# The triangular solve of the RWKV mixer in 32 by 32 blocks on the four diagonal tiles of the array

## The chip, the cores and the metric

The kernel runs on one core of one Trainium2 chip. The metric is the device time in microseconds from the first to the last instruction of a run, lower is better.

## The reference, cut to what matters

A sequence of 256 tokens with 1024 features goes through four layers; the first begins with an RWKV-7 time mix of eight heads of 64 features. Its recurrence is

```python
def step(S, inp):
    r_t, w_t, k_t, v_t, kk_t, a_t = inp
    sa = jnp.einsum('bhvk,bhk->bhv', S, -kk_t)
    S = (S * w_t[:, :, None, :] + sa[..., None] * (kk_t * a_t)[:, :, None, :]
         + v_t[..., None] * k_t[:, :, None, :])
    return S, jnp.einsum('bhvk,bhk->bhv', S, r_t)
_, o = lax.scan(step, S0, (tm(rh), tm(wh), tm(kh), tm(vh), tm(kk), tm(ah)))
```

The kernel does it in two chunks of 128 tokens (n = 0, 1). In a chunk, the vectors sa of all tokens solve (I - L) sa = x with a strictly lower triangular L of 128 by 128 for each head. So the inverse T of a unit triangular matrix is wanted, for two chunks and eight heads. What stands behind it (attention, feed-forward layers with 22 tiles each, a second network) is the bulk of the kernel and is not touched.

## The kernel before, in words

Each engine has a program of its own, written out in order; semaphores tie them together. The function tensor_program issues the matmuls, vector_program and scalar_program copy results out of the eight PSUM banks, gpsimd_program fills buffers with zeros or unit matrices. A bank is opened for a key such as ("T", i, n) when its last reader is through (opened, read_out); bank_plan fixes which key has which bank.

The inverse is built by doubling. T starts as the unit matrix with the entries of L next to the diagonal (level 0). Level i doubles the size of the solved blocks: Y = L T is formed, only the part under the mask of the level is copied (VectorE, copy_predicated into a unit matrix), and T becomes T Y. The function blocks forms one such product for one chunk: for each of eight heads (g = 0, 1 and j = 0 to 3) two matmuls of 64 by 64 on the two diagonal tiles of the array, partitions 0 to 63 and 64 to 127. Levels 1 to 5 give the inverse of each block of 64. Two last products (keys Y64 and TT64) form the block of 64 by 64 that is left of 128, with L12, the part of L between the two halves. The level's steps are, on the engines:

- TensorE: Y for n = 0 and 1, then rest(i - 1), eight matmuls of 128 columns for products that the solve itself doesn't need, then T for n = 0 and 1.
- ScalarE: copies T to Tc (L1454). VectorE: copies Y (L1961), copies rest out (L1954), turns Tc into TTc in blocks of 32 by 32 (L1974). GpSimd: a fresh unit matrix into the buffer of Y.
- Level 5 forms T and its transpose TT (both by blocks), and copies TT into TTm, whose blocks the later products use.

Ahead of the levels stand the products for L (L2362, called gram below), the turned v (L2370), turned Bt and Kt (L2378) and cross (L2386), which makes L12. Behind the last level come Y64 (L2459), rest(5), X (L2441), TT64 (L2472), and then the first matmuls of the output projection (L1109), which fill the time between the small products.

All operands of the solve are f32; each such matmul stands in the trace as two records of TensorE (and two weight loads), so that 16 matmuls are 32 records. Matmuls of fp32r operands have one.

## Time and profile before

| | |
|---|---|
| median of 3 runs | 1253.51 us (1252.48 to 1256.44) |
| profiled execution, first to last instruction | 1253.0 us |
| its own device time | not given apart; its span is 0.5 us under the median of the runs |
| TensorE busy | 1230.9 us, 98% |
| solve, from gram to the first matmul of the output projection | 93.28 to 132.51 us |
| granted TensorE clock, mean | 0.999 |

Busy is the time in which at least one instruction of the engine runs. Matmuls overlap on the array, so a busy TensorE is not one at its peak; the pace is read from the starts and the counts of records.

### The profile page before, as it was taken

The page shows a single profiled execution, that of the slowest core. Times are in us where ns is not written, and L with a number is a line of the kernel's source. Part 1 is how long each engine was busy: PE and PEld are TensorE (multiplying, and loading weights), DVE is VectorE, ACT ScalarE, POOL GpSimd, SP SyncE. Part 2 cuts the span into 40 slices and gives each one's busy share as a digit, 9 for nine tenths or more (in the row PEclk, how much of TensorE's full clock was granted, in tenths as well). Part 3 has the DMA queues.
Part 4 walks back from the last instruction along what each step waited for, and adds up shares of the span by engine and source line. Part 5 has one row for each costly group of instructions (what it writes and reads, how often), then busy time and mean ns, then how long its engine had stood idle before and what let it go on. Part 6 is the DMA issues. An engine that isn't in the chain of part 4 may idle for free.

```text
span 1253.0 us, 23639 instructions
## 1 busy us (share of the span) xinstructions
PE 1230.9 (98%) x9987; PEld 1147.4 (92%) x9987; DVE 933.6 (75%) x1260; ACT 703.9 (56%) x1032; POOL 20.1 (2%) x31
## 2 busy tenths in 40 slices
PE   6999999999999999999999999999999999999998
PEld 6999889999999879999988998999998998999997
DVE  5888369888758777999987566899976666677453
ACT  6843477555555767666657556634445554643432
POOL 0002000000000000000000000000000000000000
PEclk9999999999999999999999999999999999999999
DMA  9450277776567256689653534899965356675540
GB/s 322 168 201 4 69 247 246 250 238 229 193 220 257 105 170 234 217 291 319 249 201 119 194 130 148 290 360 351 343 234 202 136 204 200 236 250 188 202 169 34
DMA packets 163683, 263.78 MB, mean 211 GB/s; under 512 B 5677, under 2 KB 98041, under 8 KB 163578
## 3 DMA queue, kind: packets, MB, share of 16 engines
q1 hardware_dynamic: 160586, 259.54, 60.3%
q10 hardware_dynamic: 2992, 2.72, 0.7%
q8 instruction: 79, 1.29, 0.4%
q14 instruction: 26, 0.21, 0.1%
HBM read 261.17 MB, written 1.05 MB: 209 GB/s over the span
## 4 chain that ended last, share of the span: by engine, by line
PE 97%; DVE 1%; ACT 1%; DMA 1%; issue 1%; SPq 0%; DVEq 0%; ACTq 0%
PE ps L1109 26%; PE ps L1080 17%; PE ps L1082 16%; PE ps L1081 16%; PE ps L847 2%; PE ps L848 2%; PE ps L849 2%; PE ps L1095 2%; PE ps L1097 2%; PE ps L1096 2%; PE ps L2397 2%; PE ps L827 1%; DMA ring<-in_ev_w_in_dram 1%; PE ps L2406 1%; PE ps L2597 1%
## 5 line engine op out<-in xcount | busy, mean ns | idle before, releaser
L623 DVE TENSOR_TENSOR wlo<-ring,whi 128x2048 fp32r<-128x2048 f32 x194 | 443.3, 2289 | 97.6 <-ACT whi L617 97.6
L1080 PE MATMUL ps<-ghi,whi 128*128 128x256 f32 x1600 | 449.0, 281 | 0.0
L1081 PE MATMUL ps<-glo,whi 128*128 128x256 f32 x1600 | 446.8, 279 | 0.0
L1082 PE MATMUL ps<-ghi,wlo 128*128 128x256 f32 x1600 | 446.5, 279 | 0.0
L617 ACT ACTIVATE whi<-ring 128x2048 fp32r<-128x2048 f32 x194 | 370.4, 1913 | 96.7 <-PE ps L1109 69.7
L1080 PEld LDWEIGHTS ps<-ghi,whi 128*128 128x128 f32 x1600 | 300.4, 188 | 2.0 <-DVE wlo L623 0.6
L1081 PEld LDWEIGHTS ps<-glo,whi 128*128 128x128 f32 x1600 | 299.7, 187 | 0.8
L1082 PEld LDWEIGHTS ps<-ghi,wlo 128*128 128x128 f32 x1600 | 300.4, 188 | 0.0
L1109 PE MATMUL ps<-whi,yhi 128*128 128x512 f32 x480 | 159.7, 396 | 0.7 <-DVE ylo L1996 0.7
L1109 PE MATMUL ps<-wlo,yhi 128*128 128x512 f32 x480 | 156.7, 390 | 0.0
L1109 PE MATMUL ps<-whi,ylo 128*128 128x512 f32 x480 | 156.6, 390 | 0.0
L1109 PEld LDWEIGHTS ps<-whi,ylo 128*128 128x128 f32 x480 | 90.1, 188 | 19.2
L1109 PEld LDWEIGHTS ps<-wlo,yhi 128*128 128x128 f32 x480 | 90.1, 188 | 18.9
L1109 PEld LDWEIGHTS ps<-whi,yhi 128*128 128x128 f32 x480 | 88.2, 188 | 20.3 <-issue 2.4
L2218 DVE SCALAR_TENSOR_TENSOR acc<-arena,small,acc 128x512 f32<-128x512 f32 x126 | 94.7, 751 | 6.4 <-DMA arena<-in_w_ada_dram 2.5
L2255 DVE SCALAR_TENSOR_TENSOR arena<-arena,cols 128x254 f32<-128x254 f32 (+1 forms) x176 | 73.9, 479 | 14.7 <-ACT arena L1770 14.2
L1774 ACT ACTIVATE arena<-ps 128x256 f32<-128x256 f32 x44 | 16.9, 384 | 111.8 <-PE ps L1082 111.8
L2270 DVE TENSOR_TENSOR ylo<-arena,yhi 128x256 fp32r<-128x256 f32 x88 | 37.1, 422 | 47.6 <-ACT yhi L1787 47.4
L847 PE MATMUL ps<-whi,ghi 128*128 128x256 f32 x224 | 63.5, 283 | 4.0 <-DVE glo L993 4.0
L1768 ACT ACTIVATE arena<-ps 128x512 f32<-128x512 f32 x44 | 26.3, 599 | 67.1 <-PE ps L1082 65.5
L849 PE MATMUL ps<-whi,glo 128*128 128x256 f32 x224 | 62.6, 279 | 0.0
L848 PE MATMUL ps<-wlo,ghi 128*128 128x256 f32 x224 | 62.5, 279 | 0.0
(314 smaller groups left out, 1575.0 us busy)
## 6 DMA issues: line engine op xcount, KB each, us to landing
arena<-in_w_ada_dram SPq DMA_DIRECT2D x48, 1024.0 KB, 6.0
ring<-in_ff_w_up_dram SPq DMA_DIRECT2D x44, 1024.0 KB, 7.6
ring<-in_w_gate_up_dram SPq DMA_DIRECT2D x44, 1024.0 KB, 7.5
ring<-in_ff_w_down_dram SPq DMA_DIRECT2D x10, 2048.0 KB, 7.9
ring<-in_w_down_dram SPq DMA_DIRECT2D x10, 2048.0 KB, 7.8
ring<-in_od_w_qkv_dram SPq DMA_DIRECT2D x6, 2048.0 KB, 8.6
ring<-in_w_qkv_dram SPq DMA_DIRECT2D x6, 2048.0 KB, 7.9
ring<-in_w_in_dram SPq DMA_DIRECT2D x6, 2048.0 KB, 8.1
```

Of the source, the lines that this page charges most:

```text
L617: e.activation(shaped(WHI[i % NB], k), v, ACT.Copy).then_inc(S["w_hi"], 1)
L623: e.tensor_tensor(shaped(WLO[i % NB], k), v, shaped(WHI[i % NB], k).bitcast(F32), ALU.subtract).then_inc(S["w_lo"], 1)
L847: e.matmul(o, h[0][:, c, t], wh, start=c == 0, stop=False)
L848: e.matmul(o, h[0][:, c, t], wl, start=False, stop=False)
L849: x = e.matmul(o, h[1][:, c, t], wh, start=False, stop=c == NK - 1)
L1080: e.matmul(o, wh, h[0][:, k, :], start=k == 0, stop=False)
L1081: e.matmul(o, wh, h[1][:, k, :], start=False, stop=False)
L1082: x = e.matmul(o, wl, h[0][:, k, :], start=False, stop=k == NK - 1)
L1109: x = e.matmul(ps[:, :], YT[l][:, src_k + i, t], w[r][:, i, 512 * h:512 * h + 512], start=first, stop=last)
L2218: e.scalar_tensor_tensor(a, AW[:, k, :], SC[:, k:k + 1], a, ALU.mult, ALU.add).then_inc(S["ada_acc"], 1)
L2255: e.scalar_tensor_tensor(t[a][:, lag:256], z[:, 256 * a:256 * a + 256 - lag], conv_col(f, 2 - lag, a * NF + p), t[a][:, lag:256], ALU.mult ...
L2270: e.tensor_tensor(YT[1][:, p % 8, :], tg[r], YT[0][:, p % 8, :].bitcast(F32), ALU.subtract).then_inc(S["y_lo"], 1)
```

## The change

Levels 1 to 4 only need blocks of 32, since a block of 64 appears first at level 5. So the function blocks now takes four matmuls of 32 by 32 for each head, one on each diagonal tile of the array (quarter), in place of two of 64 by 64. Tc, TTc, LTc and the buffers of Y are packed to half the columns (256 for a chunk), and copies and turns go over 256 columns. The products for L are made in blocks of 32 too. Level 5 is written out apart: cross also makes LX, the part of L between two neighbouring blocks of 32; last_y forms LX T for the two pairs, last_t forms only the block below the diagonal of T and of its transpose, and TT is no longer formed in full. Copies on ScalarE put the blocks of 32 together into T64 (for Y64) and TTm. rest(5) now stands ahead of Y64, and VectorE makes P2 at level 3 in place of level 5.

```diff
         for n in range(2):
             P.use(("T", i, n), r())
-            if i == 5:
-                P.use(("TT", i, n), r())
...
-        Tc, TTc, LTc = heads64(sv(41, 1024)), heads64(PR[:, 4224:5248]), heads64(PR[:, 0:1024])
-        Yb = [heads64(PR[:, 5312:6336]), heads64(PR[:, 1088:2112])]
+        def heads32(x):
+            return [x[:, 256 * n:256 * n + 256].rearrange("p (g j c) -> p g j c", g=2, j=4) for n in range(2)]
+
+        Tc, TTc, LTc = heads32(sv(41, 512)), heads32(PR[:, 4224:4736]), heads32(PR[:, 0:512])
+        Yb = [heads32(PR[:, 5312:5824]), heads32(PR[:, 1088:1600])]
+        LX = heads32(PR[:, 512:1024])
+        T64 = [PR[:, s:s + 512].rearrange("p (g j c) -> p g j c", g=2, j=4) for s in (4736, 5824)]
...
                 eye(flat64(TTc[n]), S["tt_eye"])
+            for n in range(2):
+                zeros64(n)
...
             for x in TTm:
-                e.memset(x[:, :, :, 0:64], 0.0).then_inc(S["tt_zero"], 1)
-            for i in (1, 2, 3):
+                e.memset(x[:, :, :, :], 0.0).then_inc(S["tt_set"], 1)
+            for i in (1, 2):
...
                     e.wait_ge(S["cross"], n + 1)
+                    e.wait_ge(S["tilted"], 6)
+                    for q in (0, 2):
+                        p = slice(32 * q, 32 * q + 32)
+                        e.activation(LX[n][p, g], c3(ps_of(key)[p, 256:384], 4), ACT.Copy)
                     e.activation(L12[n][0:64, g], c3(ps_of(key)[0:64, 0:256], 4), ACT.Copy).then_inc(bank_sem(key), 1)
...
+            def blocks_of(key):
+                return ps_of(key)[:, 0:256].rearrange("p (g j c) -> p g j c", g=2, j=4)
+
+            for i in range(1, 5):
                 for n in range(2):
                     key = ("T", i, n)
                     e.wait_ge(S["t_mm"], 2 * (i - 1) + n + 1)
-                    e.activation(Tc[n], heads_of(key), ACT.Copy).then_inc(bank_sem(key), 1)
-                    if i == 5:
-                        key = ("TT", i, n)
-                        e.wait_ge(S["tt_mm"], n + 1)
-                        ps = heads_of(key)
-                        e.wait_ge(S["tt_zero"], n + 1)
-                        e.activation(TTm[n][0:64, :, :, 0:64], ps[0:64], ACT.Copy)
-                        e.activation(TTm[n][64:128, :, :, 64:128], ps[64:128], ACT.Copy).then_inc(bank_sem(key), 1)
+                    e.activation(Tc[n], blocks_of(key), ACT.Copy).then_inc(bank_sem(key), 1)
+            def laid(n, q):
+                c = slice(32 * q, 32 * q + 32)
+                e.wait_ge(S["tt_set"], 2 + n + 1)
+                e.wait_ge(S["tt_turned"], 2 * 3 + n + 1)
+                e.activation(TTm[n][c, :, :, c], TTc[n][c], ACT.Copy).then_inc(S["tt_laid"], 1)
+
+            for n in range(2):
+                e.wait_ge(*read_out(("T", 4, n)))
+                e.wait_ge(S["tt_set"], 2)
+                for q in range(2):
+                    c = slice(32 * q, 32 * q + 32)
+                    e.activation(T64[n][c, :, :, c], Tc[n][c], ACT.Copy).then_inc(S["t64"], 1)
+            for n in range(2):
+                for q in (2, 3):
+                    laid(n, q)
+            for n in range(2):
+                key = ("T", 5, n)
+                ps = blocks_of(key)
+                e.wait_ge(S["t_mm"], 8 + n + 1)
+                e.activation(T64[n][32:64, :, :, 0:32], ps[32:64], ACT.Copy).then_inc(S["t64"], 1)
+                e.activation(TTm[n][64:96, :, :, 96:128], ps[64:96], ACT.Copy)
+                e.activation(TTm[n][0:32, :, :, 32:64], ps[0:32], ACT.Copy).then_inc(bank_sem(key), 1)
+            for n in range(2):
+                for q in (0, 1):
+                    laid(n, q)
...
-                    l, lt = (c3(ps_of(key)[:, 256 * i:256 * i + 256], 4) for i in range(2))
+                    l, lt = (c3(ps_of(key)[:, 128 * i:128 * i + 128], 4) for i in range(2))
                     e.wait_ge(S["gram"], n + 1)
                     e.wait_ge(S["t_eye"], n + 1)
                     e.wait_ge(S["tilted"], 6)
                     e.wait_ge(S["tt_eye"], 2 + n + 1)
-                    e.copy_predicated(LTc[n][:, g], mask64(C_S64, 4), lt)
-                    e.copy_predicated(Tc[n][:, g], mask64(C_Y64, 4), l)
-                    e.copy_predicated(TTc[n][:, g], mask64(C_P64, 4), lt).then_inc(bank_sem(key), 1)
+                    e.copy_predicated(LTc[n][:, g], mask32(C_S32, 4), lt)
+                    e.copy_predicated(Tc[n][:, g], mask32(C_Y32, 4), l)
+                    e.copy_predicated(TTc[n][:, g], mask32(C_P32, 4), lt).then_inc(bank_sem(key), 1)
...
             for i in range(1, 6):
                 for n in range(2):
-                    key = ("Y", i, n)
+                    key, y = ("Y", i, n), Yb[(i - 1) % 2][n].rearrange("p g j c -> p (g j) c")
                     e.wait_ge(S["y_mm"], 2 * (i - 1) + n + 1)
-                    e.wait_ge(S["y_eye"], 2 * (i - 1) + n + 1)
-                    e.copy_predicated(Yb[(i - 1) % 2][n].rearrange("p g j c -> p (g j) c"), mask64(C_Y64 + 64 * i, 8),
-                                      c3(ps_of(key)[:, :], 8)).then_inc(bank_sem(key), 1)
-                if i == 5:
+                    if i < 5:
+                        e.wait_ge(S["y_eye"], 2 * (i - 1) + n + 1)
+                        e.copy_predicated(y, mask32(C_Y32 + 32 * i, 8), c3(ps_of(key)[:, 0:256], 8)).then_inc(bank_sem(key), 1)
+                        continue
+                    for q in (1, 3):
+                        p = slice(32 * q, 32 * q + 32)
+                        x = e.tensor_copy(y[p], c3(ps_of(key)[p, 0:256], 8))
+                    x.then_inc(bank_sem(key), 1)
+                if i == 3:
...
+            quarter = [slice(32 * q, 32 * q + 32) for q in range(4)]
             e.wait_ge(S["tilted"], 3)
             for n in range(2):
                 ps = [opened(e, ("L", n, g)) for g in range(2)]
                 for j in range(4):
-                    for x, y, c in ((At, Bt, 0), (Bt, At, 256)):
-                        for b in range(2):
+                    for x, y, c in ((At, Bt, 0), (Bt, At, 128)):
+                        for p in quarter:
                             for g in range(2):
-                                z = e.matmul(ps[g][half[b], c + 64 * j:c + 64 * j + 64], x[half[g], j, n, half[b]],
-                                             y[half[g], j, n, half[b]], start=True, stop=True)
+                                z = e.matmul(ps[g][p, c + 32 * j:c + 32 * j + 32], x[half[g], j, n, p], y[half[g], j, n, p],
+                                             start=True, stop=True)
                 z.then_inc(S["gram"], 1)
...
                 ps = [opened(e, ("L12", n, g)) for g in range(2)]
                 for j in range(4):
                     for g in range(2):
-                        x = e.matmul(ps[g][half[0], 64 * j:64 * j + 64], Bt[half[g], j, n, half[0]],
-                                     At[half[g], j, n, half[1]], start=True, stop=True)
+                        e.matmul(ps[g][half[0], 64 * j:64 * j + 64], Bt[half[g], j, n, half[0]],
+                                 At[half[g], j, n, half[1]], start=True, stop=True)
+                for j in range(4):
+                    for q in (0, 2):
+                        for g in range(2):
+                            x = e.matmul(ps[g][quarter[q], 256 + 32 * j:288 + 32 * j], Bt[half[g], j, n, quarter[q]],
+                                         At[half[g], j, n, quarter[q + 1]], start=True, stop=True)
                 x.then_inc(S["cross"], 1)
 
...
                 ps = opened(e, key)
                 for g in range(2):
                     for j in range(4):
-                        c = 256 * g + 64 * j
-                        for b in range(2):
-                            x = e.matmul(ps[half[b], c:c + 64], l[half[b], g, j, :], r[half[b], g, j, :], start=True, stop=True)
+                        c = 128 * g + 32 * j
+                        for p in quarter:
+                            x = e.matmul(ps[p, c:c + 32], l[p, g, j, :], r[p, g, j, :], start=True, stop=True)
                 x.then_inc(sem, 1)
...
+            def last_y(n):
+
+                ps = opened(e, ("Y", 5, n))
+                for g in range(2):
+                    e.wait_ge(*read_out(("L12", n, g)))
+                for g in range(2):
+                    for j in range(4):
+                        c = 128 * g + 32 * j
+                        for q in (0, 2):
+                            x = e.matmul(ps[quarter[q + 1], c:c + 32], LX[n][quarter[q], g, j, :], Tc[n][quarter[q], g, j, :],
+                                         start=True, stop=True)
+                x.then_inc(S["y_mm"], 1)
+
+            def last_t(n, y):
+
+                ps = opened(e, ("T", 5, n))
+                for g in range(2):
+                    for j in range(4):
+                        c = 128 * g + 32 * j
+                        for a, b in ((1, 0), (3, 2)):
+                            e.matmul(ps[quarter[b], c:c + 32], y[quarter[a], g, j, :], TTc[n][quarter[a], g, j, :],
+                                     start=True, stop=True)
+                        x = e.matmul(ps[quarter[1], c:c + 32], TTc[n][quarter[1], g, j, :], y[quarter[1], g, j, :],
+                                     start=True, stop=True)
+                x.then_inc(S["t_mm"], 1)
+
             for i in range(1, 6):
                 y = Yb[(i - 1) % 2]
                 for n in range(2):
                     for g in range(2):
                         e.wait_ge(*(read_out(("L", n, g)) if i == 1 else read_out(("T", i - 1, n))))
-                    blocks(("Y", i, n), LTc[n], Tc[n], S["y_mm"])
+                    if i == 5:
+                        last_y(n)
+                    else:
+                        blocks(("Y", i, n), LTc[n], Tc[n], S["y_mm"])
                     if i == 1:
                         if n == 0:
                             turned_in(0, Bt)
@@ -2423,9 +2496,11 @@
                     e.wait_ge(*read_out(("Y", i, n)))
                     if i > 1:
                         e.wait_ge(S["tt_turned"], 2 * (i - 2) + n + 1)
-                    blocks(("T", i, n), TTc[n], y[n], S["t_mm"])
                     if i == 5:
-                        blocks(("TT", i, n), y[n], TTc[n], S["tt_mm"])
+                        last_t(n, y[n])
+                    else:
+                        blocks(("T", i, n), TTc[n], y[n], S["t_mm"])
+            rest(5)
...
                 for g in range(2):
                     e.wait_ge(*read_out(("L12", n, g)))
-                e.wait_ge(*read_out(("T", 5, n)))
+                e.wait_ge(S["tt_set"], 2)
+                e.wait_ge(S["t64"], 4 + n + 1)
...
-                e.wait_ge(*read_out(("TT", 5, n)))
+                e.wait_ge(*read_out(("T", 5, n)))
+                e.wait_ge(S["tt_laid"], 2 * n + 2)
...
                 e.wait_ge(*read_out(("TT64", n)))
-                e.wait_ge(S["tt_zero"], 2)
+                e.wait_ge(S["tt_laid"], 4 + 2 * n + 2)
```

TensorE from the products for L to the first T. Rows are line, operation, result and operands by name, shape of the result, and count in a row. Before:

```order
L2362 MATMUL ps<-mix 64x64 x64
L2370 MATMUL ps<-consts_sb,mix 128x128 x8
L2397 MATMUL ps<-solve,pre 64x64 x16
L2378 MATMUL ps<-consts_sb,mix 128x128 x8
L2386 MATMUL ps<-mix 64x64 x8
L2397 MATMUL ps<-solve,pre 64x64 x16
L2386 MATMUL ps<-mix 64x64 x8
L2406 MATMUL ps<-mix 128x128 x8
L2397 MATMUL ps<-pre 64x64 x32
```

and in the change:

```order
L2401 MATMUL ps<-mix 32x32 x128
L2409 MATMUL ps<-consts_sb,mix 128x128 x8
L2441 MATMUL ps<-solve,pre 32x32 x32
L2417 MATMUL ps<-consts_sb,mix 128x128 x8
L2425 MATMUL ps<-mix 64x64 x8
L2430 MATMUL ps<-mix 32x32 x16
L2441 MATMUL ps<-solve,pre 32x32 x32
L2425 MATMUL ps<-mix 64x64 x8
L2430 MATMUL ps<-mix 32x32 x16
L2450 MATMUL ps<-mix 128x128 x8
L2441 MATMUL ps<-pre 32x32 x64
```

The products for L and each Y and T have twice as many matmuls of a quarter of the size, and the two cross have a second group of 16.

TensorE from the T of level 4 to TT64, just ahead of the output projection. Before:

```order
L2397 MATMUL ps<-pre 64x64 x32
L2397 MATMUL ps<-solve,pre 64x64 x32
L2406 MATMUL ps<-mix 128x128 x8
L2397 MATMUL ps<-pre 64x64 x64
L2459 MATMUL ps<-solve,pre 64x64 x16
L2406 MATMUL ps<-mix 128x128 x8
L2441 MATMUL ps<-mix,solve 64x64 x16
L2472 MATMUL ps<-solve,pre 64x64 x16
```

and in the change, where the group of the two kinds of row behind rest(4) comes 16 times:

```order
L2441 MATMUL ps<-pre 32x32 x64
L2463 MATMUL ps<-solve,pre 32x32 x32
L2450 MATMUL ps<-mix 128x128 x8
L2474 MATMUL ps<-pre 32x32 x2
L2476 MATMUL ps<-pre 32x32
...
L2450 MATMUL ps<-mix 128x128 x8
L2535 MATMUL ps<-pre 64x64 x16
L2516 MATMUL ps<-mix,solve 64x64 x16
L2548 MATMUL ps<-solve,pre 64x64 x16
```

The 32 matmuls of the last Y are now 32 of 32 by 32, the 64 of T and TT at level 5 are 48 of 32 by 32, and rest(5) has moved ahead of Y64.

ScalarE from the first copy of T to the copies of Y64. Before:

```order
L1454 ACTIVATE solve<-ps 128x512 x9
L1460 ACTIVATE solve<-ps 64x8x64
L1461 ACTIVATE solve<-ps 64x8x64
L1454 ACTIVATE solve<-ps 128x512
L1460 ACTIVATE solve<-ps 64x8x64
L1461 ACTIVATE solve<-ps 64x8x64
L1465 ACTIVATE pre<-ps 64x512 x2
```

and in the change:

```order
L1469 ACTIVATE solve<-ps 128x256 x8
L1481 ACTIVATE pre<-solve 32x8x32 x4
L1474 ACTIVATE solve<-pre 32x8x32 x4
L1489 ACTIVATE pre<-ps 32x8x32
L1490 ACTIVATE solve<-ps 32x8x32
L1491 ACTIVATE solve<-ps 32x8x32
L1489 ACTIVATE pre<-ps 32x8x32
L1490 ACTIVATE solve<-ps 32x8x32
L1491 ACTIVATE solve<-ps 32x8x32
L1474 ACTIVATE solve<-pre 32x8x32 x4
L1498 ACTIVATE pre<-ps 64x512 x2
```

Eight copies of 512 columns are copies of 256, and between the last of them and the copies of Y64 stand 18 copies of 32 partitions by 256 elements, where before there were two more of T and four into TTm.

## Rows read from the trace of the kernel before

**Rows 1.** The page: span, engines, the chain that ended last
```profile
span 1253.0 us, 23639 instructions
...
PE 1230.9 (98%) x9987; PEld 1147.4 (92%) x9987; DVE 933.6 (75%) x1260; ACT 703.9 (56%) x1032; POOL 20.1 (2%) x31
...
PE 97%; DVE 1%; ACT 1%; DMA 1%; issue 1%; SPq 0%; DVEq 0%; ACTq 0%
```
**Rows 2.** Windows: stretch, length, busy time (instructions) by engine, granted TensorE clock
```profile
93.28:95.60 2.32, 2.32 (x129) 2.13 (x128) 1.34 (x4) 0.84 (x2) 2.18 (x3) 1.00 0.13 40
...
102.78:107.78 5.00, 5.00 (x147) 4.81 (x145) 4.04 (x6) 1.19 (x2) 1.22 (x2) 1.00 0.01 3
...
132.51:162.18 29.67, 28.98 (x318) 22.76 (x317) 12.62 (x13) 14.42 (x19) 0.00 (x0) 1.00 0.27 88
```
**Rows 3.** Timeline of TensorE in the solve: start, us, line, tile shape, records
```profile
93.28 2.39 PE L2362 MATMUL ps<-mix 64*64 64x64 f32 x128
...
126.55 1.85 PE L2459 MATMUL ps<-solve,pre 64*64 64x64 f32 x29
...
129.42 1.15 PE L2441 MATMUL ps<-mix,solve 128*64 128x64 f32 x32
130.50 2.07 PE L2472 MATMUL ps<-solve,pre 64*64 64x64 f32 x32
...
143.29 0.69 PE L2446 MATMUL ps<-solve,mix 64*64 64x64 f32 x32
```
**Rows 4.** Timeline of one level on all engines, with what ended their waits
```profile
102.78 2.08 PE L2397 MATMUL ps<-pre 64*64 64x64 f32 x64
...
103.98 0.60 ACT L1454 ACTIVATE solve<-ps 128x512 f32<-128x512 f32 x1 [1.52 <-PE ps L2397]
...
104.61 0.71 DVE L1974 STREAM_TRANSPOSE pre<-solve 128x512 f32<-128x512 f32 x1 [0.36 <-ACT solve L1454]
...
104.70 2.06 PE L2397 MATMUL ps<-solve,pre 64*64 64x64 f32 x64
...
106.17 1.35 DVE L1961 COPY_PREDICATED pre<-consts_sb,ps 128x512 f32<-128x512 uint32 x2
...
106.69 1.16 PE L2406 MATMUL ps<-mix 64*128 64x128 f32 x16
```
**Rows 5.** TensorE groups by shape: count, busy us, mean ns; loads as min/median/max
```profile
L2397 PE MATMUL ps<-pre 64*64 64x64 f32 x384 | 12.3, 219 | 0.0
...
L2406 PE MATMUL ps<-mix 64*128 64x128 f32 x96 | 7.0, 285 | 0.0
...
L2684 PEld LDWEIGHTS ps<-acc,consts_sb x80: 106/108/109, 238.4 to 858.3; 128*32 128x32 f32 x80
...
L2397 PEld LDWEIGHTS ps<-pre x384: 129/135/135, 102.8 to 126.4; 64*64 64x64 f32 x192
```
**Rows 6.** Groups of ScalarE and VectorE by shape: count, busy us, mean ns
```profile
L1438 ACT ACTIVATE pre<-ps 64x256 f32<-64x256 f32 x4 | 1.3, 371 | 0.8 <-PE ps L2386 0.8
...
L1936 DVE COPY_PREDICATED pre<-consts_sb,ps 128x256 f32<-128x256 uint32 x4 | 1.7, 435 | 0.0
...
L1967 DVE SCALAR_TENSOR_TENSOR mix<-mix,cols 128x256 f32<-128x256 f32 x4 | 1.7, 478 | 0.0
```
**Rows 7.** Timelines: the last mix of v on VectorE; two copies of cross on ScalarE
```profile
94.26 0.87 DVE L1822 SCALAR_TENSOR_TENSOR mix<-ps,cols,mix 128x255 f32<-128x255 f32 x2 [2.98 <-ACT mix L1344]
...
100.41 0.64 ACT L1438 ACTIVATE pre<-ps 64x256 f32<-64x256 f32 x2
```
**Rows 8.** Transfers of the solve, 93.28 to 132.51 us: packets, MB, share
```profile
q8 instruction: 8, 0.13, 1.4%
```

More of the change, by code:

```diff
@@ L34 @@
 C_CEN = C_US + 128
-C_E64 = C_CEN + 128
-C_S64 = C_E64 + 64
-C_P64 = C_S64 + 64
-C_Y64 = C_P64 + 64
-NC = C_Y64 + 6 * 64
+C_E32 = C_CEN + 128
+C_S32 = C_E32 + 32
+C_P32 = C_S32 + 32
+C_Y32 = C_P32 + 32
+NC = C_E32 + 9 * 64
 def const_table():
@@ L59, in const_table @@
     c[:, C_CEN:C_CEN + 128] = (p == j) - (p // 64 == j // 64) / 64
-    r, j = p % 64, np.arange(64)[None, :]
-    c[:, C_E64:C_E64 + 64] = r == j
-    c[:, C_S64:C_S64 + 64] = j > r
-    for i in range(6):
+    r, j = p % 32, np.arange(32)[None, :]
+    c[:, C_E32:C_E32 + 32] = r == j
+    c[:, C_S32:C_S32 + 32] = j > r
+    for i in range(5):
         m = 1 << i
-        c[:, C_Y64 + 64 * i:C_Y64 + 64 * i + 64] = (r // (2 * m) == j // (2 * m)) & (r // m % 2 == 1) & (j // m % 2 == 0)
-    c[:, C_P64:C_P64 + 64] = (r // 2 == j // 2) & (r % 2 == 0) & (j % 2 == 1)
+        c[:, C_Y32 + 32 * i:C_Y32 + 32 * i + 32] = (r // (2 * m) == j // (2 * m)) & (r // m % 2 == 1) & (j // m % 2 == 0)
+    c[:, C_P32:C_P32 + 32] = (r // 2 == j // 2) & (r % 2 == 0) & (j % 2 == 1)
     return c
@@ L755, in mask, with mask32 @@
             return rep(CT[:, c:c + 128].bitcast(U32), 4)
-        def mask64(c, n):
-            return rep(CT[:, c:c + 64].bitcast(U32), n)
+        def mask32(c, n):
+            return rep(CT[:, c:c + 32].bitcast(U32), n)
         tg = [area(i, 256) for i in range(4)]
@@ L1288, in eye, with zeros64 @@
             def eye(x, sem):
-                e.tensor_copy(x, rep(CT[:, C_E64:C_E64 + 64], 8)).then_inc(sem, 1)
+                e.tensor_copy(x, rep(CT[:, C_E32:C_E32 + 32], 8)).then_inc(sem, 1)
             def flat64(x):
                 return x.rearrange("p g j c -> p (g j) c")
+            def zeros64(n):
+                e.memset(flat64(T64[n]), 0.0).then_inc(S["tt_set"], 1)
             e.wait_ge(S["consts_in"], 16)
@@ L1448, in heads_of @@
                 return ps_of(key)[:, :].rearrange("p (g j c) -> p g j c", g=2, j=4)
-            for i in range(1, 6):
+            def blocks_of(key):
+                return ps_of(key)[:, 0:256].rearrange("p (g j c) -> p g j c", g=2, j=4)
+            for i in range(1, 5):
                 for n in range(2):
@@ L2458, in tensor_program @@
                         c = 256 * g + 64 * j
-                        x = e.matmul(ps[half[1], c:c + 64], L12[n][half[0], g, j, :], Tc[n][half[0], g, j, :], start=True,
+                        x = e.matmul(ps[half[1], c:c + 64], L12[n][half[0], g, j, :], T64[n][half[0], g, j, :], start=True,
                                      stop=True)
                 x.then_inc(S["y64_mm"], 1)
-            rest(5)
             x_of(0)
```

## The prediction

> **What bounds the kernel now.** I read the page first: TensorE is busy for 1230.9 of 1253.0 us, and the chain that ended last is TensorE for 97% [rows 1]. Whatever the solve takes less of TensorE's time shortens the kernel, if nothing else ends later. Then the windows by stage: in gram and in the first level TensorE has no idle time at all, while in a level of 5.00 us VectorE is busy for 4.04 and ScalarE for 1.19, and behind the solve TensorE again works 28.98 of 29.67 us [rows 2]. In the solve almost nothing is loaded, so no weight is waited for there. The sum is therefore one of TensorE's pace, with a look at the copies that a faster TensorE would have to wait for.
>
> **The pace of small matmuls.** The timeline gives it: the busy time of a row less one record, over the count less one. A record of 64 by 64 lasts 0.219 us [rows 5]. TT64 and Y64 use one tile of the array: Y64's 29 records take 1.85 us, so (1.85 - 0.22) / 28 = 58 ns each. T uses two tiles: (2.08 - 0.22) / 63 = 29.5 ns [rows 4]. L2446 uses four: 32 records in 0.69 us, 15.2 ns [rows 3]. So a tile takes 58 ns for each record whatever the others do, and tiles run side by side. For 128 columns, rest (two tiles) has (1.16 - 0.285) / 15 = 58 ns, 117 ns a tile [rows 4, 5]. 128 columns cost 117, 64 cost 58; on that line 32 cost about 30 ns a tile, and four tiles give one record each 7.5 to 8 ns. That nothing else holds the records up at this pace is not shown by any row: the fastest long run is gram, four tiles, 128 records in 2.32 us, 18 ns [rows 2]. The nearest rows for the low end are the weight loads: 108 ns with 32 columns, 135 with 64, so half the columns take 27 ns off one [rows 5]. I take 8 ns, and keep 18 ns as the bad end: no long run of this trace is faster, and more records are asked for than before.
>
> The Trainium skill (TensorE: Matmul & The Clock Gate, section "Back-to-back issue gap", and TensorEngine Tiling, section "Instruction Overhead") speaks against the change: start to start is never below about 25 ns or 60 cycles, however few the columns. The trace disagrees as far as different tiles are concerned, with its 15.2 ns; for one tile, 30 ns would not break the rule. By 25 ns for every record the sum below would come out some 14 us slower.
>
> **The change part by part**, at 8 ns a record (four tiles), and 16 ns where only two tiles are used.
>
> *Ahead of the first T (93.28 to 102.78).* Gram has 256 records, 2.0 us in place of 2.32. What follows, the turned v, waits for v itself, whose last mix ends at 94.26 + 0.87 = 95.13 [rows 7], so at most 0.35 us are won. The two first Y have 64 records each in place of 32: 2 x (0.96 - 0.51) = 0.9 less. Each cross gets 32 records more, 0.26 us, so 0.5 in all. And the array changes its shape more often: L2441 has 32 records with two tiles, 32 x 29.5 = 0.94, but takes 1.08 from its start to the next group [rows 3], so a change costs about 0.15 us. There are four more here, 0.6. Sum: -0.35 - 0.9 + 0.5 + 0.6 = -0.15. ScalarE has eight more small copies at the cross, each at most the 0.37 us of 64 x 256 [rows 6], 3 us, while it waits 1.52 us before its first copy of T; I expect it to be through just in time, and at worst 0.3 us late. I count 0 for the whole.
>
> *Three levels, from the T of level 1 to that of level 4.* A level now takes 5.00 us: T 1.92, Y 1.99, rest 1.09 [rows 2, 4]. In the change TensorE has 4 x 64 records at 8 ns, 2.05, and rest with its change of shape 1.09 + 0.15. Then a wait appears. Now T for n = 0 begins at 102.78 and has its last record at about 103.74; ScalarE starts its copy at 103.98 and takes 0.60, and Y begins at 104.70, 0.12 behind its end [rows 4]. So from the last record of T to the next Y it is 0.24 + 0.60 + 0.12 = 0.96, just what T for n = 1 covers. In the change the copy has half the columns, 0.37 [rows 6], so 0.73, and T for n = 1 covers only 0.51: 0.2 us of idle TensorE in each level. Level: 2.05 + 1.24 + 0.2 = 3.5. VectorE has two turns and two copies of Y of half size, 0.43 each [rows 6], and rest's two of full size, 1.35 as Y's two now [rows 4]: some 2.7 with its starts overlapped, less than 3.5, and it is done before T asks. At level 3 the four steps of P2 (0.48 each, [rows 6]) come in: VectorE reaches 4.4 us in that level. The next T would start 3.5 us later and needs the turn and Y only by then; I find it ready 0.1 us ahead, so no stall, and 0.5 at worst. Gain: 3 x (5.00 - 3.5) = 4.5.
>
> *From the T of level 4 (117.77) to the output projection (132.51)*, 14.74 us now. After: T, wait and Y5 as above, 1.24 to the first Y5 and 2 x 0.51 for 64 records on two tiles, 2.3; rest(4) 1.24; T at level 5, 96 records on three tiles of 16 records each for a chunk, 2 x 0.51 = 1.0; rest(5) 1.24; Y64 1.87 + 0.15, X 1.08, TT64 2.0 [rows 3]. Sum 10.9, gain 3.9. The biggest part is that 128 records of T and TT at two tiles, 3.8 us, become 1.0. ScalarE could be the one that ends last: 18 copies of 256 elements from 1.65 us on. Two in a row took 0.64 with 0.37 for one [rows 6, 7], so 0.27 to 0.37 each, 4.9 to 6.7, then the copy of Y64 0.6: 7.2 to 8.9 us behind the start of T. TT64 needs it at 8.9. So at the bad end it just fits.
>
> *Supply.* Gram has 18 ns a record where four tiles gave 15 in the short run; over 128 records 0.37 us were lost somewhere. The solve has only 8 fetches of instructions [rows 8] and will have some 13. I add 0.2 us for each block of 64 matmuls that runs with four tiles, half of them behind waits: +0.9.
>
> Sum: 0 - 4.5 - 3.9 + 0.9 = -7.5 against the span of 1253.0. The median of the runs is 0.5 over that span, so 1253.5 - 7.5 = 1246.0 us. What stands behind the solve keeps its order, its loads start from the same events, and TensorE bounds it now, so the gain is not given back.
>
> **Rivals.**
>
> *The pace is not 8 but between 11.5 and 14.5 ns*, because instructions of weights and matmuls can't come faster. For it speaks gram's 18 ns against 15.2, against it that the short run shows no such limit. The stretch has 1504 records of the new kind; each ns costs, where TensorE does not wait anyway, about 1.3 us: levels 3 x 0.256, gram 0.26, tail 0.2, cross and the first Y 0.13. At 12.5 ns the gain is 7.5 - 5.9 = 1.6, time 1252. Chance 0.2. (The 25 ns of the Trainium skill, TensorE: Matmul & The Clock Gate, "Back-to-back issue gap", would be this case if it held for a matmul of two records; the trace has 30 ns for such a matmul on four tiles, so no run of before excludes it.)
>
> *Slower: the stream of records is bound at gram's 18 ns.* Then gram takes 4.6 (+2.3), the first Y and cross +1.9, a level 4.6 + 1.24 = 5.85 (+0.85 three times), while the tail has 2.3 + 1.15 + 1.7 in place of 7.7 and one more change of shape, -2.4. Sum +4.4, time 1258. It decides from 14.5 ns on, where the change gains nothing. Chance 0.1.
>
> *The copies set the end*: ScalarE's small copies take 0.45 in place of 0.37 with their partitions at 32 and their strides, and VectorE stalls level 4 by 0.5. Then 18 x 0.1 = 1.8 and 0.5 come back: time 1248.5. Chance 0.12; most of it lies in the range.
>
> *The clock falls.* It is granted in full in the solve [rows 2]. With a fourth of each tile's size and small waits in each level it could go to its lower level, 1.2 GHz; 22 us of matmuls would double: +14 us, time 1268. Against it speaks that the four small tiles of gram kept it at 1.00 [rows 2]. Chance 0.03.
>
> **How the numbers follow.** The forecast, a pace of 7.5 to 11 ns with or without 1 us of copies, has 0.55, its own range is 1244 to 1249. With the copies 0.12, the middling pace 0.2, the slow pace 0.1, the clock 0.03. For 8 in 10 the range goes from 1243.5 (no loss of supply, 8.4 gained, and 1 us more) up through the middling pace to 1252.5. About 0.3%, 3.8 us, is what a measurement of this kernel can tell from no change. Faster than that is under 1249.7: the forecast, the copies and a little of the middling pace, 0.68. Within it 0.2, slower by more 0.12 (the slow pace, the clock).
>
> **What would show it right or wrong.** Rows of Y and T with 64 records for a chunk in about 0.7 us busy, and 3.5 us from one level's T to the next. An idle TensorE of 0.2 us before each Y, ended by ScalarE's copy of T. The step T and TT at level 5 about 1.1 us in place of 3.8. Gram about 2.0 us; if it takes over 3.7, the stream of instructions is the bound and the forecast falls. If TT64 is seen to wait for ScalarE, the small copies were costed too low. A granted clock under 1.00 between 93 and 125 us would be the last rival.

## The result, and the profile after

The changed kernel takes 1276.27 us (1275.75 to 1279.25, 4 runs) against 1254.88 us: ratio 1.0184, 95% interval 1.017 to 1.0197. It is slower by 1.8%, where 0.6% faster was forecast. The page of after:

```profile
span 1274.3 us, 25019 instructions
...
PE 1238.6 (97%) x10659; PEld 1152.5 (90%) x10659; DVE 928.4 (73%) x1262; ACT 708.1 (56%) x1052; POOL 18.7 (1%) x31
...
PEclk9997699999999999999999999999999999999999
...
PE 94%; DMA 2%; issue 1%; ACT 1%; DVE 1%; SPq 0%; DVEq 0%; ACTq 0%
```

Against [rows 1] there are 672 more records on TensorE, 7.7 us more of busy time although each is smaller, and a line of the clock with two slices at 0.7 and 0.6. The timeline of TensorE in after shows the first loss (start, length, line, tile, records; in brackets the idle time ahead and what ended it):

```profile
91.33 1.17 PE L2401 MATMUL ps<-mix 64*32 64x32 f32 x115
93.41 1.33 PE L2401 MATMUL ps<-mix 64*32 64x32 f32 x127 [0.90 <-issue]
97.23 0.35 PE L2401 MATMUL ps<-mix 64*32 64x32 f32 x14 [2.49 <-issue]
...
107.26 1.11 PE L2441 MATMUL ps<-pre 32*32 32x32 f32 x101
109.44 0.41 PE L2441 MATMUL ps<-pre 32*32 32x32 f32 x26 [1.07 <-issue]
...
109.70 1.22 PE L2441 MATMUL ps<-solve,pre 32*32 32x32 f32 x97
113.20 0.44 PE L2441 MATMUL ps<-solve,pre 32*32 32x32 f32 x28 [2.29 <-issue]
113.57 1.37 PE L2450 MATMUL ps<-mix 64*128 64x128 f32 x16
114.87 1.38 PE L2441 MATMUL ps<-pre 32*32 32x32 f32 x83
117.35 0.80 PE L2441 MATMUL ps<-pre 32*32 32x32 f32 x43 [1.10 <-issue]
...
121.11 0.85 PE L2441 MATMUL ps<-solve,pre 32*32 32x32 f32 x46 [1.83 <-issue]
...
128.36 1.07 PE L2441 MATMUL ps<-solve,pre 32*32 32x32 f32 x64 [2.17 <-issue]
...
134.96 0.74 PE L2463 MATMUL ps<-solve,pre 32*32 32x32 f32 x20 [1.18 <-issue]
```

TensorE stands still in the middle of a step, ahead of instructions that wait for nothing ("issue"), and mostly about 127 records after the last time: 28 + 16 + 83 between the holes that end at 113.20 and at 117.35. A record is a load and a matmul, so that is 256 instructions with a wait or two. Such restarts come 3.8 to 4.2 us apart (93.41 and 97.23; 109.44, 113.20, 117.35 and 121.11). The next two come after twice as many records, 254 and 252, and after 7.25 and 6.60 us (128.36, 134.96), 3.6 and 3.3 us for each 256 instructions. From 97.23 to 134.96 it is 3.8 us in the mean (1266 records, 9.9 times 256 instructions, in 37.73 us). The instruction transfers of the same 59 us are as many as such blocks, 1753 x 2 / 256 = 13.7:

```profile
q8 instruction: 14, 0.23, 1.6%
```

Between holes the pace is the forecast one: (1.17 - 0.20) / 114 = 8.5 ns a record.

The windows of after show the second loss (the solve, the four stretches of it at the lower clock, and the one behind it; busy times, then the granted clock):

```profile
91.33:150.61 59.28, 45.65 (x1753) 41.86 (x1753) 22.53 (x52) 19.15 (x49) 8.92 (x12) 0.72 0.02 4
97.31:100.72 3.41, 3.41 (x29) 3.35 (x29) 1.29 (x6) 0.60 (x1) 0.00 (x0) 0.50 0.02 5
114.37:124.61 10.24, 7.30 (x332) 6.53 (x332) 5.24 (x11) 0.77 (x2) 1.33 (x3) 0.50 0.02 5
128.03:131.44 3.41, 3.08 (x84) 2.82 (x88) 0.44 (x1) 0.00 (x0) 0.00 (x0) 0.50 0.02 5
134.85:150.61 15.76, 15.65 (x244) 14.72 (x245) 3.51 (x6) 8.06 (x20) 0.00 (x0) 0.50 0.01 3
150.61:155.33 4.72, 4.72 (x12) 3.75 (x12) 2.05 (x1) 2.50 (x2) 0.00 (x0) 0.50 0.00 0
```

The solve, from gram to the output projection, takes 59.28 us in place of 39.23. Of it TensorE is idle 59.28 - 45.65 = 13.6. It is busy for 3.41 + 7.30 + 3.08 + 15.65 = 29.4 us at 0.50, the lower level, 1.2 GHz; half of that, 14.7, is an estimate of what the same matmuls would take less at the full clock. Without both the solve would be 59.3 - 13.6 - 14.7 = 31.0 us. The forecast without its term for supply was 39.2 - 8.4 = 30.8. The two parts are not the two causes, though: where TensorE stands still for instructions anyway, a faster clock would for the most part only lengthen the wait. Behind the solve 4.72 us more run at 0.50, 2.4 lost. Ahead of it after is 1.95 us early, because in before the clock was at 0.83 between 70 and 80 us and here it was not; such a stretch comes and goes from run to run, so the runs below are compared by the length of their solve, gram's first record to the projection's first.

### The profile page after: what moved, and what is told of

Same layout as the page of the kernel before. It is cut to its first block, busy times and chain, and to the rows that moved or that the text cites. A ratio compares the mean times of both kernels' runs of the same rounds, so it can differ in the third digit from the quotient of the medians.

```text
span 1274.3 us, 25019 instructions
## 1 busy us (share of the span) xinstructions
PE 1238.6 (97%) x10659; PEld 1152.5 (90%) x10659; DVE 928.4 (73%) x1262; ACT 708.1 (56%) x1052; POOL 18.7 (1%) x31
## 4 chain that ended last, share of the span: by engine, by line
PE 94%; DMA 2%; issue 1%; ACT 1%; DVE 1%; SPq 0%; DVEq 0%; ACTq 0%
PE ps L1112 26%; PE ps L1083 16%; PE ps L1085 16%; PE ps L1084 16%; PE ps L850 2%; PE ps L851 2%; PE ps L852 2%; PE ps L1098 2%; PE ps L1100 2%; PE ps L1099 2%; DMA ring<-in_ev_w_in_dram 2%; PE ps L2441 1%; PE ps L830 1%; PE ps L2450 1%; DVE wlo L621 1%
## 5 line engine op out<-in xcount | busy, mean ns | idle before, releaser
L1112 PEld LDWEIGHTS ps<-whi,yhi 128*128 128x128 f32 x480 | 88.7, 189 | 20.4 <-issue 2.4
L2293 DVE SCALAR_TENSOR_TENSOR arena<-arena,cols 128x254 f32<-128x254 f32 (+1 forms) x176 | 73.9, 479 | 14.7 <-ACT arena L1803 14.2
```

The lines of the kernel that those rows point to most:

```text
L1112: x = e.matmul(ps[:, :], YT[l][:, src_k + i, t], w[r][:, i, 512 * h:512 * h + 512], start=first, stop=last)
L2293: e.scalar_tensor_tensor(t[a][:, lag:256], z[:, 256 * a:256 * a + 256 - lag], conv_col(f, 2 - lag, a * NF + p), t[a][:, lag:256], ALU.mult ...
```

## Experiments

Theory A: TensorE's instructions arrive in pages of 256, one in about 4 us; the change uses 13.7 pages where before used 8.5. The clock follows from the idle time. Rival B: the small tiles themselves are slow. Rival C: the small tiles bring the clock down, and that is the loss.

**a2_pairs**: half the instructions for the same columns, copies and waits.

```diff
-                    for j in range(4):
+                    for j in range(0, 4, 2):
...
-                            x = e.matmul(ps[p, c:c + 32], l[p, g, j, :], r[p, g, j, :], start=True, stop=True)
+                            x = e.matmul(ps[p, c:c + 64], l[p, g, j, :], r[p, g, j:j + 2, :], start=True, stop=True)
```

> The changed kernel, with each matmul of gram and of the four packed levels taking two heads' moving blocks (64 columns) with one head's weights: half the instructions for the same columns, tiles, copies and waits (the products of other heads are not those of the reference). Theory A, supply: TensorE gets its instructions in pages of 256, one page in 3.8 us at best, and stands still when it has used one up sooner. 640 records fewer are 1280 instructions, 5 pages, 5 x 3.8 = 19 us: 1253 to 1258 us, a level of 4.3 us in place of 7.6, and almost no idle time that ends with an issue. Rival B, the array: 32 by 32 tiles have a pace of their own whatever the number of instructions, since the columns stay the same: 1270 us or more, level over 6.5. Rival C, only the lower clock costs: it stays lower with small tiles, 1270 or more and 0.5 granted in levels 2 to 5.

**a4_fours**: the same with `range(0, 4, 4)`, `c:c + 128` and `j:j + 4`.

> The same with four heads' blocks (128 columns) for one head's weights: a quarter of the instructions of the packed steps, the same columns (with the same change of the products). Theory A: a level is 64 + 16 records, 0.6 page, 2.4 us, so the copies and waits bound it at 3.5 to 3.8 us, as the prediction worked it out; 1245 to 1250 us. Rival B: no change to speak of, 1270 or more. If A is right but the waits were costed too low, levels of 4 to 4.5 us and 1250 to 1254.

Measured 1249.99 and 1247.34 us, before 1253.76 beside them. Windows of a2_pairs (the solve) and of a4_fours (the solve), then a level of a4_fours in the timeline:

```profile
90.38:127.42 37.04, 30.57 (x1113) 26.95 (x1112) 21.93 (x52) 18.82 (x49) 8.93 (x12) 1.00 0.03 9
```

```profile
93.91:124.75 30.84, 28.72 (x794) 24.81 (x793) 20.97 (x52) 18.80 (x49) 8.93 (x12) 1.00 0.02 6
```

```profile
106.43 1.07 PE L2441 MATMUL ps<-pre 32*32 32x128 f32 x32
107.62 1.07 PE L2441 MATMUL ps<-solve,pre 32*32 32x128 f32 x32
108.62 1.16 PE L2450 MATMUL ps<-mix 64*128 64x128 f32 x16
109.71 1.08 PE L2441 MATMUL ps<-pre 32*32 32x128 f32 x32
```

With the same tiles and columns the solve falls from 59.28 to 37.04 and 30.84 us, and the clock is full throughout. B falls, and C in the form that small tiles alone bring the clock down. a2_pairs came out 3 us faster than the range expected for it; it still has holes of 0.5 to 1.6 us that end with "issue", and they did not lower its clock. a4_fours has one such hole, 0.80 us behind gram. A level of a4_fours is 109.71 - 106.43 = 3.3 us, for which 3.5 were forecast; between T's busy time and Y's are 107.62 - 107.50 = 0.12 us, for which 0.2 was forecast.

**b_pace**: the kernel before, with runs of matmuls ahead of gram between which nothing waits. In each the next differs in the columns:

```diff
+            for i in range(64):
+                for p in quarter:
+                    e.matmul(z[p, 0:64], At[p, i % 4, 0, p], Bt[p, i % 4, 0, 0:64], start=True, stop=True)
+            for i in range(64):
+                for p in quarter:
+                    e.matmul(z[p, 0:32], At[p, i % 4, 0, p], Bt[p, i % 4, 0, 0:32], start=True, stop=True)
```

> The kernel before with runs of extra matmuls ahead of gram, nothing waiting between them: four diagonal 32 by 32 tiles with 256 columns (128 records), 128 columns (256), 64 columns (512), 32 columns (512), then one 64 by 64 tile with 64 columns (128). By the pace of a tile alone the runs take 7.5, 7.5, 7.7, 4.1 and 7.4 us. Theory A: a page of 256 instructions (128 records) takes at least 3.8 us: 7.5, 7.5, 15.2, 15.2 and 7.4 us, the third and fourth with holes of 1 to 3 us once in 128 records and the tile's own pace between them. Rival B: 64 and 32 columns run at one steady slower pace without holes. Clock: if small tiles alone bring it down, it falls in the first run, which has no holes; if idle time does, only in the third and fourth.

The timeline of TensorE in b_pace:

```profile
94.40 7.11 PE L2360 MATMUL ps<-mix 32*32 32x256 f32 x128
101.33 7.17 PE L2363 MATMUL ps<-mix 32*32 32x128 f32 x256
108.31 1.83 PE L2366 MATMUL ps<-mix 32*32 32x64 f32 x115
110.94 1.99 PE L2366 MATMUL ps<-mix 32*32 32x64 f32 x128 [0.80 <-issue]
114.95 1.99 PE L2366 MATMUL ps<-mix 32*32 32x64 f32 x128 [2.02 <-issue]
118.95 1.99 PE L2366 MATMUL ps<-mix 32*32 32x64 f32 x128 [2.02 <-issue]
...
130.68 1.93 PE L2369 MATMUL ps<-mix 32*32 32x32 f32 x128 [2.07 <-issue]
134.69 1.93 PE L2369 MATMUL ps<-mix 32*32 32x32 f32 x128 [2.08 <-issue]
138.41 0.43 PE L2369 MATMUL ps<-mix 32*32 32x32 f32 x13 [1.80 <-issue]
138.77 13.80 PE L2371 MATMUL ps<-mix 64*64 64x64 f32 x127
```

and windows of it (the 64 columns; one round of the 32 columns; the one tile at the end):

```profile
108.31:123.11 14.80, 7.95 (x519) 7.31 (x515) 0.00 (x0) 0.00 (x0) 0.00 (x0) 1.00 0.02 4
126.68:130.68 4.00, 1.93 (x128) 1.79 (x128) 0.00 (x0) 0.00 (x0) 0.00 (x0) 0.50 0.01 4
138.77:152.27 13.50, 13.50 (x132) 13.50 (x127) 0.00 (x0) 0.00 (x0) 0.00 (x0) 0.50 0.01 2
```

This is the limit by itself: 128 records restart every 4.00 us (110.94, 114.95, 118.95; 130.68, 134.69), once after 3.72 (138.41), with 64 columns as with 32. The run of 128 columns, 28 ns a record and so 3.5 us for 128, has no hole; it probably lives on pages that came during the slower run ahead of it. In gram of before, the starts of the records have one gap of 0.19 us behind the 114th; after has its first hole behind the 115th. So gram's 18 ns for 15.2 [rows 2, 3] was probably a small sign of the same limit. The clock went as neither expectation had it: with 64 columns it stayed full in spite of the holes, with 32 columns it fell, and the run of one tile then took 13.80 us in place of 7.4.

The Trainium skill (Runtime: NRT & Kernel Launch, section "Instruction fetch mechanics") describes these pages, 16 KiB blocks of 256 instructions, the next fetched while the current one runs, and calls the cost of crossing one mostly hidden. The sizes agree with the holes; the cost does not, 2.0 us for every 4.0 here. Its rule of about 25 ns from one matmul to the next at 64 columns or fewer (TensorE: Matmul & The Clock Gate, "Back-to-back issue gap"), weighed in the prediction, does not hold across four tiles: 8.5 ns.

**af_wide** and **af_half**: work is added in the solve, one wide matmul (128 columns of weights, 512 columns) ahead of each step Y and T, or of each Y alone.

```diff
+            def wide(key):
+                ps = opened(e, key)
+                e.matmul(ps[:, :], CT[:, C_CEN:C_CEN + 128], CT[:, 0:512], start=True, stop=True)
...
+                    wide(("Y", i, n))
...
+                    wide(("T", i, n))
```

> The changed kernel with one more matmul of 128 by 128 by 512 ahead of each of the 20 steps Y and T of the solve, into the bank that the step writes anyway: 20 x 0.88 = 17.6 us of work for 40 records, 0.3 of a page. Theory A: it is done while the next page comes, a level stays at 7.6 to 8 us at the full clock, and if the clock had fallen because TensorE stood idle, it is now granted in full: 1268 to 1280 us. If the clock falls for the small tiles themselves, it stays at 0.5 in part of the solve and the wide matmuls cost double there: 1285 and more. Rival B, the array's pace: the work adds to it, 1276 + 17.6 = 1294.

> The changed kernel with a matmul of 128 by 128 by 512 ahead of the 10 steps Y alone: 8.8 us of work where af_wide had 17.6. In af_wide levels took 8.05 us and TensorE was busy nearly all of it, so they were bound by the added work and the pages about equally. Theory A: with half the added work a level is bound by its 2.15 pages, 7.6 to 8.2 us, and the time is 1266 to 1272 if the clock holds, 1272 to 1278 if it falls again. If holes were no matter of supply but a fixed cost of the steps, the time would drop by the whole 8.8 us, to 1264.

Measured 1272.74 and 1275.04 us. Windows of three levels of af_wide:

```profile
107.43:115.48 8.05, 8.05 (x283) 4.73 (x281) 3.11 (x6) 1.52 (x5) 0.80 (x2) 1.00 0.02 4
115.48:124.15 8.67, 8.01 (x282) 4.80 (x280) 3.64 (x8) 0.77 (x2) 0.80 (x2) 1.00 0.01 4
124.15:132.20 8.05, 8.05 (x282) 4.73 (x281) 4.05 (x9) 0.77 (x2) 0.95 (x1) 1.00 0.02 4
```

17.6 us of added work (20 matmuls) leave the solve at 59.44 us, as long as without them (59.28), in levels of 8.05, 8.67 and 8.05 us where after has 7.6, 9.0 and 7.5. The holes are filled but for one of 0.67 us, and the clock stays at 1.00 there, with the small tiles in place. TensorE is busy for all of the two shorter levels, so there its work takes as long as the pages do and sets the length as well. af_half separates them: with half the work the solve is 58.36 us, only 1.1 us shorter, and holes and a second stretch at the lower clock are back (mean clock 0.94). So small tiles alone did not lower the clock of after, and the length is that of the pages. What lowers it is not settled: it fell next to holes in after, and did not in a2_pairs and in the 64 columns of b_pace, which have holes too.

**a_y2** and **a_gram** ask for the dose and for gram alone.

> The changed kernel with two heads' blocks for one head's weights in the steps Y of levels 1 to 4 alone (products of other heads are not the reference's): 208 records a level, between the 272 of the changed kernel and the 144 of a2_pairs, for the same columns. Theory A, a page of 128 records in 3.9 us: a level of 1.65 pages takes 6.4 us, and 4 x 64 = 256 records fewer are 2 pages, 8 us: 1266 to 1270 us, a little less if the clock falls for a shorter time. If holes came per step and not per page, the levels stay at 7.6 or fall to 4.5 at once.

> a4_fours with gram as the change has it, 256 records of 32 columns (levels keep a quarter of the instructions, with the same change of their products). It prices gram alone: in a4_fours gram took 1.96 us with 64 records. Theory A: 256 records are two pages behind the one that is there, two holes of 1 to 2.5 us, 6 to 6.5 us in all, and the clock may fall for the turned v behind it, 1.5 us: 1251 to 1254 us, 4 to 6 over a4_fours. If gram is paid by records alone (10 ns), 1248.

Measured 1272.01 and 1257.22, before 1255.65 beside them. Both missed the expected range on the high side, a_gram by less than its second stretch at the lower clock costs (6.8 us, below); that the clock is the reason in a_y2 too is argued and not shown. Windows of a_gram (gram; the step T of level 5; what follows it):

```profile
90.74:97.30 6.56, 2.72 (x257) 2.46 (x256) 2.16 (x8) 0.84 (x2) 5.41 (x6) 1.00 0.09 26
...
119.51:122.12 2.61, 1.32 (x98) 1.20 (x96) 1.78 (x4) 2.47 (x7) 0.00 (x0) 1.00 0.00 0
122.12:135.77 13.65, 13.65 (x124) 12.57 (x119) 1.33 (x2) 7.59 (x14) 0.00 (x0) 0.50 0.01 2
```

Gram alone goes from 1.96 to 6.56 us, about as expected. What was not expected: its 192 more records shift where a page ends, a hole of 1.3 us now falls into T of level 5, and behind it the clock is at 0.50 for 13.65 us of work that has no hole at all, some 6.8 us. In a_y2 the solve is 54.72 us with 1498 records, 4.6 less than after for 255 fewer records, where 8 were expected; TensorE's mean clock is 0.74 there.

| kernel | records in the solve | pages x 4.0 us | solve, us | mean clock |
|---|---|---|---|---|
| a4_fours | 794 | 24.8 | 30.84 | 1.00 |
| before | 1082 | 33.8 | 39.23 | 1.00 |
| a2_pairs | 1113 | 34.8 | 37.04 | 1.00 |
| a_y2 | 1498 | 46.8 | 54.72 | 0.74 |
| after | 1753 | 54.8 | 59.28 | 0.72 |
| af_wide | 1793 | 56.0 | 59.44 | 0.97 |

No solve is shorter than its pages (records x 2 / 256 x 4.0). A level of before had 0.5 us to spare (144 records, 4.5 of 5.00 us). After up to 134.85 has 1509 records in 43.5 us, where the pages are 47 at 4.0 us and 45 at the 3.8 us measured there: the length is that of supply, less what was probably in store at the start. The work in it would take 45.65 - 15.65 - 6.9 = 23.1 us at the full clock (6.9 is half of the 13.8 at 0.50), so up to 20.4 us are the price of supply, of which 13.6 show as idle time in the whole solve. The last 15.76 us have 244 records, and there the clock is the price, 7.8 us.

**p1_last**: the kernel before with the new fifth level alone, levels 1 to 4 at 64 by 64.

```diff
+                    if i == 5:
+                        last_y(n)
+                    else:
+                        blocks(("Y", i, n), LTc[n], Tc[n], S["y_mm"])
...
-                        blocks(("TT", i, n), y[n], TTc[n], S["tt_mm"])
+            rest(5)
```

> The kernel before with the fifth level alone in the new form: Y of level 5, T and its transpose form only the 32 by 32 block below (above) the diagonal, on 32 by 32 tiles, with rest(5) right behind; gram, levels 1 to 4 and all layouts stay at 64 by 64. Y5, T5 and TT5 have 64 + 96 records where before had 64 + 128, so instructions get fewer, not more. Working: Y5 1.99 becomes 2 x 0.6 with waits 1.4, T5 and TT5 3.75 become 1.3, one or two more changes of shape, some wait for ScalarE's six copies. Theory A (supply by pages): no added page, gain 2 to 3.5 us: 1250.5 to 1252.5. If the packed form itself is what costs, wherever it stands (rival B), no gain: 1253.5 or more.

1264.82 us, ratio 1.0084 (1.0065 to 1.0102): slower by 0.8%, and the expectation missed. Timelines of p1_last on VectorE, GpSimd and TensorE:

```profile
123.73 1.67 DVE L1977 SCALAR_TENSOR_TENSOR mix<-mix,cols 128x256 f32<-128x256 f32 x4
126.52 1.33 DVE L1958 COPY_PREDICATED mix<-consts_sb,ps 128x512 f32<-128x512 uint32 x2 [1.11 <-POOL mix L1321]
...
125.47 0.95 POOL L1321 MEMSET mix<- 128x1024 f32 x1 [14.24 <-DVE mix L1977]
...
128.00 2.08 PE L2416 MATMUL ps<-mix 64*128 64x128 f32 x16 [3.54 <-DVE mix L1958]
130.01 3.67 PE L2501 MATMUL ps<-solve,pre 64*64 64x64 f32 x32
```

I had left P2 at level 5 and moved rest(5) ahead of Y64. rest(5) needs a bank that VectorE empties behind P2 and GpSimd's memset, so TensorE waits 3.54 us. Y64, 2.08 us in a4_fours, then takes 3.67: the clock is at the lower level for the rest of the solve, which is 45.31 us long with fewer records (1049) than before.

**p2_last** puts both right.

```diff
-                if i == 5:
+                if i == 3:
                     for j in range(4):
                         e.wait_ge(*read_out(("rk", j // 2)))
```

> p1_last with its idle time taken away: P2 is made at level 3 and rest(5) stands behind Y64 again as in the kernel before, ScalarE's copies for TT are ordered so that what Y64 and TT64 need comes first. In p1_last TensorE stood 3.5 us ahead of rest(5) for VectorE, behind P2 and GpSimd's memset, and the clock was then at 0.50 for 17 us. If that wait and the clock that followed it were the whole loss, the new fifth level gives back about 2 us: 1251 to 1252.5 us, clock full in the solve. If the loss lay in the packed form, it stays: 1258 or more. If only the wait goes and the clock still falls, 1256 to 1260.

**v_wide** tries to keep the packed 32 columns with half the instructions, by weights that hold two blocks:

```diff
-                        for p in quarter:
+                        for p in half:
                             x = e.matmul(ps[p, c:c + 32], l[p, g, j, :], r[p, g, j, :], start=True, stop=True)
...
-                        blocks(("T", i, n), TTc[n], y[n], S["t_mm"])
+                        blocks(("T", i, n), T64[n], y[n], S["t_mm"])
```

> The changed kernel with the same products but half the instructions in them: the weights of a step are 64 by 64 with two 32 by 32 blocks on their diagonal and zeros beside them, the moving side stays in packed 32 columns, so one matmul forms two blocks; ScalarE lays the turned T out for it, four copies of 0.38 us a level. 144 records a level as in the kernel before, of which 128 with 32 columns. Theory A: what counts is the number of instructions, so it behaves as a2_pairs did: levels of 4.0 to 4.7 us, bound by 1.15 pages, holes of at most 1.5 us, clock full, 1249.5 to 1252.5 us, faster than before by 1 to 4 us. If ScalarE's copies hold T up, levels over 5 us and 1254 or more. Rival B (the 32-column pace itself): over 1265.

p2_last: 1253.0 us, ratio 0.999 (0.9982 to 0.9999). Its solve is 36.81 us, 2.4 less than before, at full clock: the fifth level's new form does gain, without the wait. The interval allows between 0.1 and 2.3 us of it in the whole time, and the median is half a microsecond above the expected range. The rest goes with the clock elsewhere: among executions with a mean clock of 1.000, p2_last takes 1250.2 us (2 of them) and before 1253.1 (14); among those with 0.998 or 0.999, 1253.2 (9) and 1255.7 (7). So at equal clock it gains 2.5 to 2.9 us, but the lower mean came in 9 of its 11 executions and in 7 of 21 of before. Whether the edit brings that is not shown. v_wide: 1252.43 us, ratio 0.9992 (0.9983 to 1.0002), solve 38.83. It is free of the loss of after, as A says, and its time lies in the expected range, but it is not shown to be faster than before, and its levels did not become shorter (4.94 us, where 4.0 to 4.7 were expected). A level of v_wide in the timeline, and the loads and matmuls of L2456 (min/median/max):

```profile
102.34 2.06 PE L2456 MATMUL ps<-pre 64*64 64x32 f32 x64
104.23 2.03 PE L2456 MATMUL ps<-solve,pre 64*64 64x32 f32 x64
...
107.28 2.06 PE L2456 MATMUL ps<-pre 64*64 64x32 f32 x64
```

```profile
L2456 PEld LDWEIGHTS ps<-pre x128: 129/135/136, 102.3 to 109.1; 64*64 64x64 f32 x128
L2456 PE MATMUL ps<-pre x128: 218/219/241, 102.3 to 109.1; 64*64 64x32 f32 x128
```

64 records take 2.06 us as with 64 columns [rows 4]: (2.06 - 0.22) / 63 = 29 ns, 58 a tile, though only 32 columns move. What sets a tile's record here is the width of its weights. The Trainium skill (TensorE: Matmul & The Clock Gate, section "LDWEIGHTS (loading the stationary operand)") says that a load takes columns / 1.2 ns, 53 ns for 64. The pace of 58 ns a tile is near it; a single load lasts longer, 135 ns in the row above. My expectation for v_wide overlooked it.

## Why the prediction was wrong

**The step that failed is "Supply".** It added 0.2 us for each block of 64 matmuls, "+0.9". The holes are 13.6 us, and supply made the stretch up to 134.85 up to 20.4 us longer than its work at the full clock. The prediction had numbers that pointed at it: gram's 18 ns against 15.2, 0.37 us lost in it, and 8 fetches in the solve [rows 8] against "some 13". It counted the fetches but gave them no rate. A level of before has 144 records in 5.00 us [rows 4]; the transfers show 8 pages in 39.23 us. That was never tested as a bound because TensorE was busy 98%, and a page every 4.9 us looks idle when its share of the queues is 1.4%.

**The rival "slower"** had the right sign and cause by name (a stream bound at gram's 18 ns), 1258 us, at 0.1. It was mis-sized: the stream is not a steady 18 ns but 8.5 ns for 128 records and then a hole, 30 to 31 ns a record in the mean (3.8 to 4.0 us for 128). That "the short run shows no such limit", held against the middling pace, was the wrong evidence, since L2446 with 32 records [rows 3] fits in a page that was there already.

**"The clock falls"** got 0.03 and was priced for "small waits in each level". It happened, in after in four stretches that begin in a hole or within 1.2 us behind one. The matmuls in them would take 14.7 us less at the full clock, but only what lies behind the last hole is surely the clock's: 7.8 us in the solve and 2.4 behind. What sets it off beside holes stays open. The argument against it, gram at 1.00, was from a run whose largest gap is 0.19 us.

**The pace of 8 ns** was right within a page (8.5), and so was its reading from two widths, though for a reason that I did not have: the change narrows the weights as well as the moving side, and v_wide, which narrows only the moving side, stays at 58 ns a tile.

**The parts**, read from a4_fours, where supply binds only in the 0.80 us behind gram: ahead of the first T 103.07 - 93.91 = 9.16 us (forecast 9.5), a level 3.3 (3.5), the tail from T of level 4, at 113.04, to 124.75, 11.7 (10.9). Their sum is 30.84, the forecast without supply 30.8. It is a stand-in: its records move 128 columns in 28 ns, 7 ns for each 32, where the change has 8.5, so the levels of the change itself would be up to 0.4 us longer each (an estimate, 256 x 1.5 ns). The tail is longer by 0.75 for a wait of rest(5) for VectorE that the prediction had not seen, the same wait that p1_last made long. The idle time ahead of Y was 0.1 to 0.2 us, as forecast (0.2). "The copies set the end" did not happen: TT64 waits 0.1 us at most. One price in the prediction is mislabelled: at its own 1.3 us for each ns, a pace of 25 ns puts the sum some 22 us higher; the 14 us that it gives are against the kernel before.

**"TensorE bounds it now, so the gain is not given back"** held in the main for a4_fours (8.4 us less in the solve, 6.4 in the whole), and says nothing where the work becomes shorter than its instructions take to arrive.

## What to carry to other kernels

Before splitting matmuls into smaller tiles, count the instructions of the stretch on the engine: on this chip, in this kernel, 256 of them (128 records of load and matmul) took 3.8 to 4.0 us to arrive, so what a record takes less than about 30 ns, or 15 ns an instruction, is not gained over a long run. It shows as idle time that "issue" ends in the middle of a step, at equal counts. And a stall in TensorE can cost twice: 3.5 us of waiting in p1_last, or a hole of 1.3 in a_gram, was followed by 13 to 17 us at half the clock. It need not: holes of up to 1.6 us in a2_pairs and of 2.0 us in b_pace left it full.

## What the runs showed of the hardware that I had not expected

- Instruction pages: one in 4.00 us in most of b_pace, where nothing else binds, and 3.8 us in the mean in after, although a page's own transfer takes less: 14 fetches are 1.6% of 16 engines' time in the 59.28 us of after's solve, about 1.1 us each. What fills the rest of the 4 us stays open.
- A tile of 64 by 64 needs 58 ns a record with 32 moving columns as with 64 (v_wide), a 32 by 32 tile 14 x 4 = 56 ns with 64 and, in after, 8.5 x 4 = 34 ns with 32: in these four forms the wider of weights and moving side counts.
- After the lower clock is granted, work without holes does not at once bring it back: L2371 of b_pace runs 13.8 us without a hole on one 64 by 64 tile at 108 ns a record, where the full clock has 58, and the run of 64 columns, with 2 us of idle time in every 4, had kept the full clock for 14.8 us. Idle time alone does not tell when it falls.
